# State-space stage: weight units in another order and in 4 KB packets, the sums of squares over 128 partitions, a third buffer for the powers of C

## The reference, cut to what matters

```
sh1, sc1, gt1, sh2, sc2, gt2 = silu(c) @ w_mod + b_mod       # w_mod: 2048 x 12288, 96 MB
h_lat = rmsnorm(x_lat, gain) * (1 + sc1) + sh1               # the same for the context
h_ctx = rmsnorm(x_ctx, gain) * (1 + csc1) + csh1
y_ctx, y_lat = s5_mixer(h_ctx, h_lat, ...)                   # two directions, complex diagonal states
```

## Time and profile before

| | |
|---|---|
| time, median of 3 runs | 3556.82 us |
| profiled execution, its own time | 3554.54 us |
| its span | 3552.7 us |
| state-space stage (to the first L439) | 465.1 us |
| engines over the span | PE 92%, DVE 60%, ACT 39%, GpSimd 14% |
| chain that ended last | PE 83%, DVE 6%, GpSimd 5%, DMA 2% |
| mean granted TensorE clock | 0.955 |

### The profile page before, as it was taken

How to read it: one execution, slowest core, us unless ns; L and a number is a source line. 1 busy time by engine, 2 the same in 40 slices (tenths; PEclk the granted TensorE clock), 3 DMA queues, 4 the chain that set the end, 5 groups by cost and what they waited for, 6 DMA issues and landing times.

```text
span 3552.7 us, 51801 instructions
## 1 busy us (share of the span) xinstructions
PE 3286.0 (92%) x21097; PEld 2763.3 (78%) x21097; DVE 2145.0 (60%) x1850; ACT 1380.7 (39%) x1385; POOL 480.5 (14%) x352
## 2 busy tenths in 40 slices
PE   5788899799999999886789999999999899999998
PEld 3445578688888888675678888888868788888887
DVE  7668755565555555699565555555644555555555
ACT  4446543433333333322234434433323344344332
POOL 2869900000000000096000000000000000000000
PEclk7888899899999999998799999999999999999999
DMA  9988875255555555344145555555524455555552
GB/s 299 305 282 257 260 243 175 91 184 189 185 189 182 190 186 189 107 142 148 36 154 178 186 190 182 186 189 189 177 92 142 142 186 184 187 187 189 189 183 89
DMA packets 351014, 643.22 MB, mean 181 GB/s; under 512 B 21599, under 2 KB 50359, under 8 KB 350519
## 3 DMA queue, kind: packets, MB, share of 16 engines
q1 hardware_dynamic: 309952, 561.68, 48.9%
q10 hardware_dynamic: 40951, 79.98, 6.6%
HBM read 637.54 MB, written 4.06 MB: 181 GB/s over the span
## 4 chain that ended last, share of the span: by engine, by line
PE 83%; DVE 6%; POOL 5%; issue 2%; DMA 2%; ACT 1%; SPq 1%; DVEq 1%; ACTq 0%; POOLq 0%
PE acc L439 49%; PE acc L440 25%; POOL cpow L1841 3%; DMA raw<-in_w_mod_dram 2%; POOL ptmp L1841 1%; PE acc L1263 1%; DVE z L943 1%; DVE w_lo L793 1%; PE acc L1280 1%; PE acc L521 1%; PE acc L533 1%; PE acc L464 1%; PE acc L1188 1%; PE acc L1247 1%; DVE hf L832 0%
## 5 line engine op out<-in xcount | busy, mean ns | idle before, releaser
L439 PE MATMUL acc<-xin,w_hi 128*128 128x512 f32 x5376 | 1915.2, 399 | 58.9 <-DVE xin L807 33.7
L793 DVE TENSOR_TENSOR w_lo<-raw,w_hi 128x2048 fp32r<-128x2048 f32 x484 | 1111.2, 2301 | 1079.0 <-ACT w_hi L640 1078.8
L440 PE MATMUL acc<-xin,w_lo 128*128 128x256 f32 x5376 | 1519.4, 283 | 0.0
L640 ACT ACTIVATE w_hi<-raw 128x2048 fp32r<-128x2048 f32 x484 | 926.8, 1917 | 1365.1 <-PE acc L440 1365.0
L439 PEld LDWEIGHTS acc<-xin,w_hi 128*128 128x128 f32 x5376 | 1017.2, 189 | 312.5 <-issue 35.6
L440 PEld LDWEIGHTS acc<-xin,w_lo 128*128 128x128 f32 x5376 | 1021.5, 190 | 0.0
L439 PE MATMUL acc<-hid,w_hi 128*128 128x512 f32 x2432 | 845.4, 392 | 0.0
L440 PE MATMUL acc<-hid,w_lo 128*128 128x256 f32 x2432 | 681.2, 280 | 0.0
L439 PEld LDWEIGHTS acc<-hid,w_hi 128*128 128x128 f32 x2432 | 455.1, 187 | 101.4
L440 PEld LDWEIGHTS acc<-hid,w_lo 128*128 128x128 f32 x2432 | 459.6, 189 | 0.0
L799 DVE TENSOR_REDUCE tmp<-acc 128x1024 f32<-128x2048 f32 x116 | 265.0, 2284 | 19.9 <-PE acc L440 19.9
(11 more groups left out here) (241 smaller groups left out, 2063.5 us busy)
## 6 DMA issues: line engine op xcount, KB each, us to landing
raw<-in_ffn_w_gate_dram SPq DMA_DIRECT2D x88, 1024.0 KB, 5.2
raw<-in_ffn_w_up_dram SPq DMA_DIRECT2D x88, 1024.0 KB, 5.1
raw<-in_ffn_w_down_dram SPq DMA_DIRECT2D x88, 1024.0 KB, 5.1
raw<-in_w_mod_dram ACTq DMA_DIRECT2D x76, 1024.0 KB, 9.7
raw<-in_w_mlp_in_dram SPq DMA_DIRECT2D x64, 1024.0 KB, 5.2
raw<-in_w_mlp_out_dram SPq DMA_DIRECT2D x64, 1024.0 KB, 5.1
raw<-in_s_w_glu_dram SPq DMA_DIRECT2D x32, 1024.0 KB, 5.3
raw<-in_ab_w_in_dram SPq DMA_DIRECT2D x32, 1024.0 KB, 5.3
```

The lines of the kernel that those rows point to most:

```text
L439: pe.matmul(bank, w_hi[:, slot, w], operand[:, kt, :], start=(kt == 0), stop=False)
L440: ins = pe.matmul(bank[:, 0:TOK], w_lo[:, slot, w], operand[:, kt, 0:TOK], start=False, stop=(kt == UK * units - 1))
L640: act.activation(w_hi[:, slot, :], raw[:, slot, :, :].rearrange("p k n -> p (k n)"), ACT.Copy).then_inc(hi_ready, 1)
L793: dve.tensor_tensor(w_lo[:, slot, :], raw[:, slot, :, :].rearrange("p k n -> p (k n)"), w_hi[:, slot, :].bitcast(F32), SUB).then_inc(lo_re ...
```

## The change

It has these parts.

1. **Units.** The blocks b = 0, 1 stay as units of 4 K-tiles by 512 columns. All 80 other units are 2 K-tiles by 1024 columns, 256 runs of 4 KB; each feeds two column blocks at once.
2. **Order.** 8 units before the loop and then 5, 6, 5, 6, ... per step (`FIRST_UNIT`), where there were 16 before it and then 4, 8, 8, 8, 8, 4, 4, .... Block b = 1, 2, 3 is finished at steps 1, 5, 7 (`COLUMNS_AT`) instead of -1, 2, 4.
3. **Norms.** `xs` is [128, 4, 2048], two DMAs of 2 MB at once, ahead of the units; four squares of 128x2048 instead of eight of 64x2048; their sums `ss_x` are turned into [64, 8] by 8 small matmuls.
4. **Third buffer.** `cpow[2]` lies in the last 8 KB of `xin` and is used up to n = 11; after that tiles alternate between two buffers again.
5. **Prologue order.** PE: `select_c(0)` first, then the norm sums, `ada_rows(0, 8)`, the columns; the states of tile 0 ahead of its lag blocks. VectorE: `modulation(0)` ahead of both rounds of powers. ScalarE: squares after all of `copy_b`. SP: units 8 to 11 behind `load_x(1)`, so behind `normalise_x(0)`.

```diff
-        xs = Region(xin_at, xin_at + 32 * KB)("xs", [64, L // 2, D])
+        xs = Region(xin_at, xin_at + 32 * KB)("xs", [P, L // 2, D])
+        cpow.append(Region(xin_at + 24 * KB, xin_at + 32 * KB)("cpow2", [P, 2, CB, L * GRP]))
+        LAST_THIRD = KT - 5
+        CPOW_OF = [n % 3 if n <= LAST_THIRD else (n - LAST_THIRD - 1) % 2 for n in range(KT)]
+        CPOW_FREE = [max([k + 1 for k in range(n) if CPOW_OF[k] == CPOW_OF[n]], default=0) for n in range(KT)]
...
+        SINGLE = [mod_block(b, v) for b in range(2) for v in range(2)]
+        PAIRS = [(mod_block(2, v), mod_block(3, v)) for v in range(2)] + [(ada_block(n), ada_block(n + 1)) for n in range(0, KT, 2)]
+        COLUMNS_AT = {1: 1, 5: 2, 7: 3}
+        FIRST_UNIT = [8 + 11 * (r // 2) + 5 * (r % 2) for r in range(KT + 1)]
+        def ada_load(queue, first, last):
+            for i in range(first, min(last, ADA_UNITS)):
+                slot = i % SLOTS
+                col, _, k = UNIT_OF[i]
+                if i >= SLOTS:
+                    queue.wait_ge(ada_unit, i - 3)
+                if i < 4 * len(SINGLE):
+                    queue.dma_start(raw[:, slot, :, :], w_mod[:, k[0]:k[0] + 4, col:col + UN]).then_inc(raw_ready[slot], 16)
+                else:
+                    queue.dma_start(raw[:, slot, :, :].rearrange("p (k h) n -> p k (h n)", h=2),
+                                    w_mod[:, k[0]:k[0] + 2, col:col + 2 * UN]).then_inc(raw_ready[slot], 16)
...
-            load_xs(0)
-            ada_units(sp, 0)
             load_c(0)
+            load_xs()
+            ada_load(sp, 0, 4)
             load_x(0)
-            sp.wait_ge(xs_sq, 4)
-            load_xs(1)
-            ada_units(sp, 1)
-            ada_units(sp, 2)
+            ada_load(sp, 4, 8)
             sp.wait_ge(c_sel, 1)
             load_c(1)
-            ada_units(sp, 3)
             sp.wait_ge(xt_scaled, 1)
             load_x(1)
+            ada_load(sp, 8, 12)
...
                 if k + 2 < KT:
                     modulate_u(k + 2, k % 2)
-                    ada_units(act, ADA[k + 1] + 1, (0, 1))
+                    i = FIRST_UNIT[k + 1]
+                    ada_load(act, i + 4, i + 6)
                 if k >= 0:
                     copy_output(k)
                 if k + 2 < KT:
                     copy_e(k + 2)
-                    ada_units(act, ADA[k + 1] + 1, (2, 3))
+                    ada_load(act, i + 6, i + 8)
                 if k + 3 < KT:
                     copy_lam_powers(k + 3)
                     normalise_x(k + 3)
-                if 0 <= k < 4:
-                    ada_units(act, ADA[k + 1] + 2)
+                if k + 2 < KT:
+                    ada_load(act, i + 8, FIRST_UNIT[k + 2] + 4)
+                if k == KT - 2:
+                    ada_load(act, FIRST_UNIT[k + 1] + 4, FIRST_UNIT[k + 2])
...
+            dve.wait_ge(ss_tr, 1)
+            dve.tensor_scalar(rstd_x[:, :], ps[2][0:64, 0:L], 1.0 / D, EPS, MUL, ADD).then_inc(ss_ready, 1)
             powers_of_b(c0, 0)
-            dve.wait_ge(xs_sq, 8)
-            dve.tensor_scalar(rstd_x[:, :], rstd_x[:, :], 1.0 / D, EPS, MUL, ADD).then_inc(ss_ready, 1)
-            powers([ab[:, 2], ab[:, 3]], uu, L)
             dve.wait_ge(rstd_root, 1)
             dve.reciprocal(rstd_x[:, :], rstd_x[:, :]).then_inc(rstd_ready, 1)
             modulation(cm, 0)
+            powers([ab[:, 2], ab[:, 3]], uu, L)
...
                 pool.wait_ge(c_sb, n + 1)
-                if n > 1:
-                    pool.wait_ge(y_done, n - 1)
+                if n == 2:
+                    pool.wait_ge(xs_sq, 4)
+                if CPOW_FREE[n]:
+                    pool.wait_ge(y_done, CPOW_FREE[n])
```

More of the change, by code:

```diff
@@ L1181, in select_c, with ada_rows @@
                 ins.then_inc(c_sel, 1)
-            def ada_rows(m, window, units=range(UK)):
-                for kk in units:
-                    pe.wait_ge(raw_ready[kk], 16 * (m + 1))
+            def ada_rows(first, last):
+                for i in range(first, last):
+                    slot = i % SLOTS
+                    _, window, k = UNIT_OF[i]
+                    pe.wait_ge(raw_ready[slot], 16 * (i // SLOTS + 1))
                     for q in range(UK):
-                        ins = pe.matmul(ps[0][32 * q:32 * q + 32, :], cond[:, kk * UK + q, window:window + 32], raw[:, kk, q, :],
-                                        start=(m + kk == 0), stop=(kk == UK - 1), skip_group_check=True)
+                        ins = pe.matmul(ps[0][32 * q:32 * q + 32, :], cond[:, k[q], window[q]:window[q] + 32], raw[:, slot, q, :],
+                                        start=(i == 0), stop=(i % 4 == 3), skip_group_check=True)
                     ins.then_inc(ada_unit, 1)
-            def mod_rows(b, v):
-                ada_rows(MOD[b][v], 47 - (16 + 4 * b + 2 * v))
             def mod_columns(b):
@@ L1302, in _ @@
             transpose_parameters()
-            mod_rows(0, 0)
-            mod_rows(0, 1)
+            pe.wait_ge(b_sb, 3)
+            select_c(0)
+            pe.wait_ge(xs_sq, 4)
+            pe.wait_ge(angle_ready, 1)
+            for f in range(4):
+                for q in range(2):
+                    ins = pe.matmul(ps[2][32 * q:32 * q + 32, 2 * f:2 * f + 2], ident[:, f:P:4], ss_x[:, 2 * q:2 * q + 2], start=True, stop=True)
+            ins.then_inc(ss_tr, 1)
+            ada_rows(0, 8)
             pe.wait_ge(b_sb, 4)
+            pe.wait_ge(c_sb, 1)
             mod_columns(0)
-            select_c(0)
-            mod_rows(1, 0)
-            pe.wait_ge(c_sb, 1)
+            pe.wait_ge(mod_raw, 1)
+            select_c(1)
             spread_modulation(0)
-            select_c(1)
             transpose_x(0)
@@ L1314, in _ @@
             transpose_e(0, 1)
-            mod_rows(1, 1)
             for k in range(-1, KT):
+                if k in COLUMNS_AT:
+                    mod_columns(COLUMNS_AT[k])
                 if k + 1 < KT:
-                    lag_blocks(k + 1, (k + 1) % 2)
+                    if k >= 0:
+                        lag_blocks(k + 1, CPOW_OF[k + 1])
                     states(k + 1, (k + 1) % 2)
+                    if k < 0:
+                        lag_blocks(0, 0)
+                    i0, i1 = FIRST_UNIT[k + 1], FIRST_UNIT[k + 2]
                 if k >= 0:
-                    outputs(k, k % 2)
+                    outputs(k, k % 2, CPOW_OF[k])
+                if k in COLUMNS_AT:
+                    pe.wait_ge(mod_raw, COLUMNS_AT[k] + 1)
                 if k + 1 < KT:
[L1324 to L1328, removed]
+                    if k in COLUMNS_AT:
+                        pe.wait_ge(ada_sb, COLUMNS_AT[k] + 1)
+                    ada_rows(i0, i0 + 2)
                 if k + 2 < KT:
@@ L1381, in copy_c, with copy_adarow @@
                                scale=-1.0).then_inc(c_sb, 1)
-            def copy_adarow(n, m):
-                act.wait_ge(ada_unit, 4 * m + 4)
+            def copy_adarow(n, units):
+                act.wait_ge(ada_unit, units)
                 if n:
@@ L1387, in copy_adarow, with square_x @@
                 act.activation(adarow[:, :], ps[0][:, :], ACT.Copy).then_inc(ada_sb, 1)
[L1389 to L1392, removed]
+            def square_x():
+                act.wait_ge(xs_in, 32)
+                for j in range(L // 2):
+                    act.activation(xs[:, j, :], xs[:, j, :], ACT.Square, accum_out=ss_x[:, j:j + 1]).then_inc(xs_sq, 1)
             def block_diagonal_b(n):
@@ L1492, in _ @@
             copy_r8(0)
-            copy_adarow(1, MOD[1][1])
             for k in range(-1, KT):
```

60 lines of the change are left out of this document (28 added, 32 removed).

## The result

The changed kernel takes 3566.56 us (median of 7 runs, 3560.75 to 3573.65) where the kernel before takes 3556.82 (7 runs, 3546.34 to 3558.98): ratio 1.0032, 95% interval 1.0021 to 1.0042. It is slower by 0.3%; forecast was a gain of 0.8%, 3529 us.

A forecast was written before the change was run, and what follows sets the result against it. Bounds: a ring through two cpow buffers in steps 5 to 13, late w_mod units in steps 1 and 2. Prologue 6 + loop 24 - end 2.6 = 27.5 us gained, profiled 3554.5 to 3527, median 3529; range 3508 to 3546.

The forecast's parts named there:

- Loop (24 us forecast): Thirteen steps from lag_blocks(2) to lag_blocks(15): 297.1 us before, 273 forecast, 24 us gained, nearly all in steps 1 to 4.
- 2.86: Loop: DMA us per 4 KB-packet unit, taken as 2.98 x 387 / 403.
- the landing bound of 268.5: Loop: units 5 and 6 are issued late, so six-unit steps take 21.9 us, five-unit ones 19.2; 268.5 with copy_adarow.
- the prediction's own DMA bound: Loop: 70 units x 2.86 plus 13 x 4.2 us of small transfers is 254.8, at 0.92 busy 277 us.
- Steps: Loop: steps were to alternate near 19.5 and 22 us, with TensorE waiting for the fifth and sixth unit.
- Prologue (6 us forecast): Before the loop: phases(0) near 81.4 against 87.8, 6 us gained, or 1 with contended prices.
- End (2.6 us lost): lag_blocks(15) to first L439: gated unit's loads share DMA with two more units; 2.6 us lost, 5.7 if last.
- GpSimd alone: Rival, chance 0.13: late units cost nothing, DMA has slack; loop 13 x 19.2 = 249.6, 51 us gained, 3506 us.
- Packets of 4 KB bring nothing: Rival, chance 0.14: units stay at 2.98 us of DMA; loop 286, 14.5 us gained, 3542 us.
- Small transfers late: Rival, chance 0.17: tw lands late behind 4 KB packets; steps 21.6 us each, 20 us gained, 3537 us.
- Units late at the low clock: Rival, chance 0.06: TensorE waits for units 5 and 6 every step, loop 316, 16 us lost, 3572 us.
- the rival's 5.0 us: Loop: 64 tw packets per engine, each alternating with a 4 KB instead of 2 KB w_mod packet, take 5.0 us more.

The follow-up runs named there:

- e1: The kernel before plus 32 bytes of padding ahead of the work region, nothing else: 3571.37 us, ratio 1.0043.
- e2: The changed kernel with ss_x at the end of the stage's own tiles, so w_hi, w_lo and hid lie where they lay before: 3547.75 us, ratio 0.9984.
- e3: e2 with every unit loaded as four K-tiles of 512 columns in 2 KB packets, same order and steps: 3549.18 us.
- e7: e2 with only the first K-tile of two loaded from unit 16 on, half the bytes, stale data for the rest: one run, 3514.95 us.
- e5: e2 with SP issuing the x loads behind the write of the next lag blocks instead of ahead: 3541.21 us, ratio 0.9957.
- e12: e5 with the units of e3, in 2 KB packets: 3549.54 us, ratio 0.9978.
- e18: The changed kernel, ss_x and SP's order untouched, padded so that weights lie 64 bytes and hid 96 bytes further up: 3520.90 us, ratio 0.99.
- e17: The kernel before with the weights w_hi and w_lo 64 bytes and hid 96 bytes further up: 3525.79 us, ratio 0.9915.

## Why the prediction was wrong

**The step that failed first was one that the prediction never wrote down.** It summed the 465 us whose instructions the diff touches and took the other 3087 as given. `ss_x` was costed at nothing, without the cover named that would hide it, and its place in the diff, ahead of `work_at`, was plain to see. It cost 14 us in e1, and taking it out gave back 19 in e2 by the medians. That turned a small gain into a loss. No rival held this case either: the one that was slower had its loss from late units and the clock.

**Loop (24 us forecast).** 297.4 us in the changed kernel's profile, 287.3 in that of e2, which has the same code but for the address; forecast 273. The two profiles stand 2.9 us above and 5.2 us below the medians of their kernels, which covers 8 of the 10 us between them, if it lies in the loop. A median run would then gain some 5 us in the loop (an estimate) and not 24. The mis-sized terms, by e2: a unit costs 2.97 us and not 2.86 (68.2 x 0.11 = 7.5 us), the small transfers 21.7% of 287.3 over 13, 4.8 us a step and not 4.2 (7.8), with 1.8 units fewer loaded than counted (-5.1). That is 10 us more of DMA work, 265 instead of 254.8, and over the 0.92 busy that was taken, 288. This agrees with 287.3 because the two queues were 0.92 busy in e2, as was taken; the prices were worked out from the same share, so it confirms no more than that. The share is no constant: 0.89 in the changed kernel, 0.96 in e3.

The second fault was to take the middle between this bound and the landing bound of 268.5. Two bounds do not average; the larger one holds. Whether the landing bound was right stays open. The loop of e7 took 266.0, but that this is near 268.5 is chance: units landed in 4.9 us there instead of 9.3, and the steps with six units took 20.0 us where the landing bound has 21.9.

The changed kernel's profile has the same DMA work (68.0% and 21.0% of 297.4 are 265 us again) and 13.0 us of waits for `tw` against 7.5. That these waits are a part of its longer loop is argued, from one profile each.

**Why 2.86 was wrong.** The ratio of the two packet sizes was right, even low: 6% (2.97 to 3.15), where 4% was taken. At fault was the price that it was applied to. 2.98 came from 140 to 250 us, four steps of which three have eight units. Over steps 5 to 13 (250.3 to 436.7) the same trace has

```profile
q10 hardware_dynamic: 19366, 38.45, 61.6%
q1 hardware_dynamic: 19996, 8.89, 22.7%
```

which is 36.7 units at 3.13 us each and 4.7 us of small transfers a step. Both are close to what the new loop showed in 2 KB packets (e3: 3.15 and 4.6). With 3.13 x 387 / 403 = 3.01 and with 4.7 the prediction's own DMA bound is 272 us of work and 295 us of loop, hardly a gain. What makes the price is argued: small transfers take 15.3% of the engines' time in rows 5, and 21 to 23% in the dearer stretches.

**Steps.** Forecast were 19.5 and 22, found in e2 20.2 with five units and 24.4 with six (means, between the starts of `lag_blocks`; 18.6 to 22.5 and 20.5 to 30.1).

**Prologue (6 us forecast).** 9.3 gained: `lag_blocks(2)` at 130.25 instead of 139.56. That is as much as the whole change gains in e2. The path to `modulation(0)` came out as worked out, the eighth unit done at 55.5 (forecast 55.5):

```profile
53.60 1.94 PE L1206 MATMUL acc<-raw,cond 128*32 128x512 f32 x8 [2.20 <-DMA raw<-in_w_mod_dram]
...
58.43 0.17 DVE L1565 TENSOR_TENSOR msum<-mraw,par 128x8 f32<-128x8 f32 x1 [11.70 <-ACT mraw L1444]
...
59.94 0.39 DVE L1565 TENSOR_TENSOR ab<-ab 128x128 f32<-128x128 f32 x1
...
67.77 1.27 DVE L1565 TENSOR_TENSOR tv<-ab,tv 128x128 f32<-128x128 f32 x4
...
78.59 1.07 POOL L1867 TENSOR_TENSOR ptmp<-ab 128x512 f32<-128x512 f32 x1 [23.64 <-DVE tv L1787]
```

The four operations that took 4.93 us beside GpSimd's work take 1.27 with GpSimd idle, as the prediction argued, and the powers begin 1.5 us after `modulation(0)` (58.43 to 59.94), where 3.0 were taken. `phases(0)` starts at 78.59, forecast 81.4.

**End (2.6 us lost).** 33.8 us, 34.2 in e2, against 28.3: 5.5 to 6 lost, about the worst case that was named. Units wait 4.14 and 1.63 us there at a granted clock of 0.75.

**The rivals.**

- *GpSimd alone*: fell; DMA has no slack (0.93 busy in e2).
- *Packets of 4 KB bring nothing*: wrong as DMA time (6%), right for the end-to-end time until the order on SP is mended (e3 against e2). The Trainium skill (DMA: Bandwidth & Descriptors, Specifications) has 512 B as enough for the full rate; under this load 4 KB packets cost 6% less than 2 KB ones, and the measurement decides.
- *Small transfers late*: right in its effect, not in its mechanism. The scratch write's landing went from 6.3 us (before, over the thirteen steps) to 9.9, `tw` from 2.6 to 6.3, and TensorE waited for `tw` as that rival said; it was forecast at 8 us beyond the main case and is worth about as much (6.5, e5). The turn-taking of queues that the Trainium skill has there (the same page, Queues, rings and completion order) fits the write: with packets half as long it lands in 7.5. It does not show for `tw`, on which the rival's 5.0 us rest: `tw` lands in 6.4 us beside 2 KB packets too (e3), in 4.0 and 4.2 with the mended order (e5, e12), and in 2.5 with half the bytes (e7). There the load and the order count, and the packet size does not.
- *Units late at the low clock*: the clock granted over the loop was 0.91 (0.90 in e2, single steps down to 0.78), so it was not what set the steps in the main; at the end, at 0.75, it may have been part of it.

None of the four had the cause of the loss, which lies outside the stage.

Put together by medians: at the places of before the change gives 9 us (e2; by its ratio 6, interval 2 to 10) and at the best places 5 (e18 against e17), where 27.5 were forecast; the shift of 32 bytes takes 19; what is left is the 10 us loss measured.

## What to carry to other kernels

Where a tile is added ahead of a region, everything in that region has a new address, and the matmuls that read it may have a new price: put it behind, and compare the mean of each untouched group before and after. When the largest stage is one group of matmuls, a few paddings of 32 to 64 bytes are the cheapest experiment there is. And of several bounds on a loop take the largest, with DMA prices from a stretch with the same mix of large and small transfers as the one to come; a saved wait is worth only what the next bound leaves, here one bound by the bytes.

## What the runs showed of the hardware

- The mean of 5376 matmuls of 128x512 on `xin` is 399 ns or 395 with the weights 64 bytes further up, and that of 2432 on `hid` 390 to 399 by both places, at the same granted clock (0.95 to 0.96 over the span). Profiles at the same places agree to 1 ns on `xin` and 2 on `hid`. Between the worst and the best pair lie 45 us of this kernel (3571.4 in e1_before_pad32, 3525.8 in e17).
- The same transfer of the same size in the same packets has no one price: a unit in 2 KB packets took 3.0 us of the DMA engines in steps 1 to 4 of the kernel before, 3.13 in its steps 5 to 13, and 3.15 in e3.
- Larger packets on one queue can make a small transfer on the other land later: a write of 120 KB in 7.5 us beside 2 KB packets (e3) and in 9.9 beside 4 KB ones (e2). Reads of 64 KB landed in 6.4 and 6.3.
- VectorE operations of 128x128 took 1.23 us each beside GpSimd's work and 0.32 without it (changed kernel, 67.77).
